# One 512-column matmul for two of the high-part terms of a split-float32 product, on one NeuronCore

## The reference, cut to what matters

```python
def conv_ffn(h, w_up, cw, cb, w_down, prev):
    u = h @ w_up                                   # 1024 -> 2 * 2816
    y, new_prev = causal_dwconv(u, prev, cw, cb)   # 3 taps along the tokens
    g, val = jnp.split(y, 2, axis=-1)
    return (jax.nn.silu(g) * val) @ w_down, new_prev
```

## Time and profile before

| | |
|---|---|
| runs of the kernel before, us | 1524.21, 1524.72, 1529.47 |
| span of the profiled execution, us | 1519.0 |
| granted TensorE clock, mean | 0.971 |
| TensorE matmuls, busy | 12097, 1413.4 us |
| VectorE busy | 976.7 us |
| ScalarE, GpSimd busy | 576.7 us, 638.5 us |

### The profile page before, as it was taken

The page is one execution under the profiler, slowest core; times in us unless marked ns, Lnnn a source line. Parts: engine busy times, 40 slices in busy tenths (PEclk is TensorE's granted clock), DMA queues, the critical chain, the costliest instruction groups (busy, mean ns, idle before and its releaser), DMA issues.

```text
span 1519.0 us, 32537 instructions
## 1 busy us (share of the span) xinstructions
PE 1413.4 (93%) x12097; PEld 1313.9 (86%) x12097; DVE 976.7 (64%) x1658; ACT 576.7 (38%) x1019; POOL 638.5 (42%) x420
## 2 busy tenths in 40 slices
PE   6986978989999999999799989999989999999997
PEld 6984758979999999999699966657889999999997
DVE  5769967576773167765748688753677761376755
ACT  4544354344432133422415235432454431234323
POOL 1586422304444334433177888402223443344430
PEclk9998789989999999999999999999999999999999
DMA  5344364213333232332145769995213233233321
GB/s 173 114 117 79 63 169 123 83 44 85 99 94 98 77 97 83 102 98 75 45 121 164 226 175 308 331 340 157 69 57 97 84 103 90 83 91 88 104 83 62
DMA packets 289082, 180.47 MB, mean 119 GB/s; under 512 B 54248, under 2 KB 274572, under 8 KB 288924
## 3 DMA queue, kind: packets, MB, share of 16 engines
q1 hardware_dynamic: 288412, 179.07, 40.9%
q10 hardware_dynamic: 576, 0.13, 0.0%
HBM read 167.10 MB, written 10.63 MB: 117 GB/s over the span
## 4 chain that ended last, share of the span: by engine, by line
PE 70%; DVE 14%; issue 8%; ACT 2%; SPq 2%; DMA 1%; POOL 1%; DVEq 0%; ACTq 0%; POOLq 0%
PE big L2649 58%; PE big L2715 3%; PE misc L2800 2%; DVE tmp L1261 2%; PE big L2746 2%; DVE y L1738 1%; DVE rstd L1219 1%; DVE x L1744 1%; DVE w_lo L1208 1%; DVE x_lo L1251 1%; SPq L597 1%; PE misc L2770 1%; ACT yc L2506 1%; DVE cp L1261 1%; ACT w_hi L2144 1%
## 5 line engine op out<-in xcount | busy, mean ns | idle before, releaser
L949 POOL TENSOR_TENSOR w_lo<-raw,w_hi 128x1024 fp32r<-128x1024 f32 (+2 forms) x153 | 393.8, 2574 | 708.9 <-ACT w_hi L2144 548.4
L2144 ACT ACTIVATE w_hi<-raw 128x1024 fp32r<-128x1024 f32 (+2 forms) x179 | 198.5, 1109 | 582.1 <-PE big L2649 539.0
L2649 PE MATMUL big<-x_hi,w_hi 128*128 128x264 f32 x1984 | 406.7, 287 | 8.4 <-DVE uc L1827 2.8
L2649 PE MATMUL big<-x_hi,w_lo 128*128 128x264 f32 x1984 | 400.8, 283 | 0.0
L2649 PE MATMUL big<-x_lo,w_hi 128*128 128x264 f32 x1984 | 398.8, 283 | 0.0
L2649 PEld LDWEIGHTS big<-x_hi,w_hi 128*128 128x128 f32 x1984 | 305.9, 189 | 13.1 <-issue 4.7
L2649 PEld LDWEIGHTS big<-x_lo,w_hi 128*128 128x128 f32 x1984 | 305.6, 189 | 0.0
L2649 PEld LDWEIGHTS big<-x_hi,w_lo 128*128 128x128 f32 x1984 | 305.3, 189 | 0.0
L1831 DVE SCALAR_TENSOR_TENSOR yc<-uc,convw,yc 128x512 f32<-128x512 f32 x88 | 136.7, 1554 | 113.2 <-ACT yc L2506 113.2
L2649 PE MATMUL big<-h_hi,w_hi 128*128 128x264 f32 x616 | 125.1, 284 | 6.3 <-DVE h_lo L1846 6.3
L2649 PE MATMUL big<-h_hi,w_lo 128*128 128x264 f32 x616 | 123.9, 282 | 0.0
(11 more groups left out here) (434 smaller groups left out, 2330.8 us busy)
## 6 DMA issues: line engine op xcount, KB each, us to landing
raw<-in_w_up SPq DMA_DIRECT2D x88, 512.0 KB, 3.9
raw<-in_w_down SPq DMA_DIRECT2D x32, 704.0 KB, 4.7
areas<-in_cache_k SPq DMA_DIRECT2D x41, 384.0 KB, 4.5
areas<-in_cache_v SPq DMA_DIRECT2D x41, 384.0 KB, 4.7
raw<-in_w_in SPq DMA_DIRECT2D x16, 512.0 KB, 4.2
raw<-in_w_out SPq DMA_DIRECT2D x16, 512.0 KB, 4.2
raw<-in_w_kv SPq DMA_DIRECT2D x12, 512.0 KB, 4.6
spare<-in_cache_k SPq DMA_DIRECT2D x12, 384.0 KB, 4.5
```

The lines of the kernel that those rows point to most:

```text
L949: pool.tensor_tensor(w_lo[slot][:, 0:kb, :], raw[slot][:, 0:kb, :], w_hi[slot][:, 0:kb, :].bitcast(F32), ALU.subtract).then_inc(lo_made, 1)
L2144: A.activation(w_hi[slot][:, 0:kb, :], raw[slot][:, 0:kb, :], ACT.Copy).then_inc(hi_made, 1)
L2649: ins = pe.matmul(big[2 * slot + b_][:, 0:c1 - c0], w[slot][:, k, :], r[:, c0:c1], start=(k == 0 and n_ == 0), stop=(k == kb - 1 and n_ == 2))
```

## The change

The high and low parts of an activation become one tensor (`x_hl`, `h_hl`, with `x_hi`, `x_lo`, `h_hi`, `h_lo` as its two views, at the same place and of the same size). For the second column part, `w_hi` meets the high and the low part in one matmul of 2 x 256 columns, whose two results stand side by side in the 512 columns of the bank. The `w_lo` term of that part goes on top of the first 256 columns. Per k there are five matmuls in place of six. The two results are added when a panel is read. `product` stays as it was for the memory panels and for `glu`, and `kvf` is unchanged too; the panels of `win0`, `wout0`, the four up and four down phases, `win1`, `kv` and `wout1` take the new form, 164 panels with 1408 k steps. Its core:

```diff
+            def term(slot, n, k, kb, hl):
+                c0, c1 = HALF[0] if n in (0, 2, 3) else HALF[1]
+                o, wide = big[2 * slot + (n in (1, 4))], c1 - c0
+                if n == 1:
+                    return pe.matmul(o[:, 0:2 * wide].rearrange("p (a t) -> p a t", a=2), w_hi[slot][:, k, :],
+                                     hl[:, :, k, c0:c1], start=(k == 0), stop=False)
+                w, part = (w_lo if n > 2 else w_hi), 1 if n == 2 else 0
+                return pe.matmul(o[:, 0:wide], w[slot][:, k, :], hl[:, part, k, c0:c1],
+                                 start=(k == 0 and n == 0), stop=(k == kb - 1 and n > 2))
...
+            LATE = HALF[1][1] - HALF[1][0]
+            def both(slot, dst):
+                src = big[2 * slot + 1][:, 0:2 * LATE].rearrange("p (a t) -> p t a", a=2)
+                return V.tensor_reduce(dst, src, AX.X, ALU.add)
...
                             dve.wait_ge(panel_done, q + 1)
-                            st(V.tensor_tensor(uu[:, 2:266], big[2 * slot][:, 0:264], rstd[:, 0:264], ALU.mult))
-                            V.tensor_tensor(uu[:, 266:2 + NT], big[2 * slot + 1][:, 0:256], rstd[:, 264:NT],
-                                            ALU.mult).then_inc(panel_read, 1)
+                            late = uu[:, 2 + HALF[1][0]:2 + NT]
+                            st(both(slot, late))
+                            st(V.tensor_tensor(uu[:, 2:2 + HALF[0][1]], big[2 * slot][:, 0:HALF[0][1]], rstd[:, 0:HALF[0][1]],
+                                               ALU.mult))
+                            sy(1)
+                            V.tensor_tensor(late, late, rstd[:, HALF[1][0]:NT], ALU.mult).then_inc(panel_read, 1)
```

```diff
-                ins = V.tensor_tensor(dst, dst, src, add) if add else V.tensor_copy(dst, src)
+                if n and add:
+                    for i in range(2):
+                        ins = V.tensor_tensor(dst, dst, big[2 * (q % 2) + 1][:, i * LATE:(i + 1) * LATE], ALU.add)
+                        if i == 0:
+                            do(ins)
+                            sync()
+                elif n:
+                    ins = both(q % 2, dst)
```

More of the change, by code:

```diff
@@ L1780, in copy_out @@
                     dve.wait_ge(panel_done, q + 1)
[L1781 to L1787, removed]
+                    first, late = (y[:, m, c0:c1] for c0, c1 in HALF)
+                    src = big[2 * (q % 2)][:, 0:HALF[0][1]]
+                    high, low = (big[2 * (q % 2) + 1][:, i * LATE:(i + 1) * LATE] for i in range(2))
+                    if add:
+                        do(V.tensor_tensor(late, late, high, ALU.add))
+                        added = own.n
+                        do(V.tensor_tensor(first, first, src, ALU.add))
+                        dve.wait_ge(dve_step, added)
+                        ins = V.tensor_tensor(late, late, low, ALU.add)
+                    else:
+                        do(V.tensor_copy(first, src))
+                        ins = both(q % 2, late)
+                    tell(ins, panel_read, q + 1)
                     for a_ in conv_rows(m) if conv is not None else ():
@@ L2636, in all_read, with joined @@
                     pe.wait_ge(free_, (jobs - n + len(frees) - 1) // len(frees))
+            def term(slot, n, k, kb, hl):
[7 more added lines that the diff above has]
+                                 start=(k == 0 and n == 0), stop=(k == kb - 1 and n > 2))
+            def joined(q, slot, kb, hl, wait_k=None, free=True, each=None):
+                pe.wait_ge(lo_made, q + 1)
+                if free:
+                    pe.wait_ge(panel_read, q - 1)
+                for k in range(kb):
+                    if wait_k is not None:
+                        wait_k(k)
+                    for n in range(5):
+                        ins = term(slot, n, k, kb, hl)
+                    if k == kb - 1:
+                        ins.then_inc(panel_done, 1)
+                    if each is not None:
+                        each(k)
             def product(q, slot, kb, rhs, cols, wait_k=None, free=True, each=None):
@@ L2656, in _, with product_by_halves, phase @@
             xs_ = lambda k: (x_hi[:, k, :], x_lo[:, k, :])
[L2658 removed]
+            def product_by_halves(q, slot, kb, hl, wait_half):
                 pe.wait_ge(lo_made, q + 1)
                 pe.wait_ge(panel_read, q - 1)
[L2662 removed]
+                for b_ in range(2):
                     wait_half(b_)
                     for k in range(kb):
[L2665 to L2668 removed]
+                        for n in ((0, 2, 3), (1, 4))[b_]:
+                            ins = term(slot, n, k, kb, hl)
                 ins.then_inc(panel_done, 1)
[L2671 removed]
+            def phase(name, hl=x_hl, wait_k=None, wait_half=None, first=0, last=0):
                 kb, n, base, _ = PH[name]
@@ L2710, in last_pair @@
                         slot = q % 2
-                        def part(k, n_):
-                            xh, xl = rhs(k)
-                            w, r = ((w_hi, xh), (w_hi, xl), (w_lo, xh))[n_]
-                            return pe.matmul(big[2 * slot + b_][:, 0:c1 - c0], w[slot][:, k, :], r[:, c0:c1],
-                                             start=(k == 0 and n_ == 0), stop=(k == kb - 1 and n_ == 2))
                         if b_ == 0:
@@ L2734, in first_pair @@
                 add = x_stats(name)
-                for b_, (c0, c1) in enumerate(HALF):
+                for b_ in range(2):
                     for p_ in range(2):
@@ L2744, in first_pair @@
                                 x_split(KD * b_ + k)
-                            for n_, (w, r) in enumerate(((w_hi, x_hi), (w_hi, x_lo), (w_lo, x_hi))):
-                                ins = pe.matmul(big[2 * slot + b_][:, 0:c1 - c0], w[slot][:, k, :], r[:, k, c0:c1],
-                                                start=(k == 0 and n_ == 0), stop=(k == KD - 1 and n_ == 2))
+                            for n_ in ((0, 2, 3), (1, 4))[b_]:
+                                ins = term(slot, n_, k, KD, x_hl)
                             if b_ == 0 and p_ == 0 and k == LAST_READ:
@@ L3267, in _ @@
             for m in range(n):
[L3268 removed]
+                joined(base + m, (base + m) % 2, kb, x_hl)
                 if m:
```

102 lines of the change are left out of this document (54 added, 48 removed).

## The result

The changed kernel takes 1667.88 us (median of 4 runs, 1663.67 to 1670.58) where the kernel before took 1524.47 (1523.25 to 1529.47): a ratio of 1.0932, 95% interval 1.09 to 1.0963. It is slower, as forecast, but by 143 us where 103 were forecast, and the time lies above the range. The profiled execution has a span of 1668.4 us, 149.4 above that of before.

The account below looks back on a forecast made before the run. Bound in the up loop: a closed VectorE-ScalarE chain, not TensorE. Span 1519.0 - 7.2 (matmuls) + 98.6 (up loop) + 3.4 (phase ends) + 8 (`kv`) = 1621.8; median 5.7 above, 1628 us, 6.8% slower; range 1572 to 1650.

Parts of the forecast that it names:

- Rival 1: Up loop: the late multiplication is not held up, TensorE's 11.35 us decides; 1513 us, faster; chance 0.13.
- Rival 2: Up loop: only the even `w_lo` holds up the late multiplication; iteration grows 1.29 us, 1576 us in all; chance 0.08.
- Rival 4: Whole kernel: the change doesn't do what it says; at most the matmuls' saving is zero, +7 us; no chance given.
- Three signs: Up loop: VectorE busy above 90%, TensorE's idle before even panels ended by `w_lo`; joined matmul start to start near 225 ns.
- In each phase I count this for nine of eleven iterations.: Four up phases: 2.74 us more in nine iterations each, +98.6 us; first and last iterations counted at nothing.
- The loop's term: Up loop: 4 x 9 x 2.74 = +98.6 us, from iterations growing to 14.27 us.
- I take 11.8, the row of the same kind.: TensorE: joining two 256-column matmuls saves one fixed part of 11.8 ns a k step.
- The 608 steps: Joined k steps outside the up phases and `kv`: 608 x 11.8 ns = -7.2 us.
- saving of 20.6 ns: TensorE, other end of the estimate: a lean joined matmul of 216 ns saves 20.6 ns a k step.
- Ends of the four phases with a norm ... +3.4: Two late readings each on VectorE's chain at phase ends: 2.3 us as additions, 1.1 as copies, +3.4 in all.
- the turns that were put at nothing: Down phases, `win0`, `win1` and the up phases' first and last iterations: no added time forecast.
- rival 3: Up loop: TensorE's idling lowers the granted clock; below 0.79 its panels show, at 0.70 1698 us; chance 0.05.

Follow-up runs that it names:

- e3: The changed kernel with the up loop's reduction `both` issued twice, with a wait between: 1680.33 us, ratio 1.1044.
- e1: The changed kernel with the up loop's late part read out of PSUM in three operations of at most one SBUF input each: 1537.21 us, ratio 1.0097.
- e5: As e1, with the late readings with `rstd` in `win0`, `kv` and `win1` also taken out of PSUM: 1529.56 us, ratio 1.0031.
- e7: Joined matmul only in up phases and down-phase panels read by copies, additions; e1's reading in up loop, rest as before the change: 1523.89 us, ratio 0.9975.
- e6: As e1, but the up loops' joined matmul reads 512 neighbouring columns in one piece (wrong columns, same count): one run, 1533.29 us.
- e2: The kernel before, six matmuls kept; up loop's late part first copied to `uc` in SBUF, then multiplied there: 1650.28 us, ratio 1.0846.
- e4: The changed kernel with each GpSimd `w_lo` subtraction split into two instructions of half the blocks, in every phase: 1586.62 us, ratio 1.0428.

## Why the prediction was right in kind and too small

**Right: the mechanism and the iteration.** The late multiplication is held up by both `w_lo` of an iteration and ends 0.28 us behind them (0.24 was assumed); the odd `w_lo` has moved to the last tap; L1831 (now L1860) runs in 0.75 us. The iteration is 14.32 us against 14.27. The reduction took 0.68 us against 0.69, and e3 shows that its price would not have mattered in the steady loop. Rival 1 fell with the changed kernel itself and its reason, that only operations of 512 and more columns had been seen blocked, fell too: one of 8 columns was stopped for 3 us (below). Rival 2 fell with the odd multiplication's 1.99 us. Rival 4 fell by the page's count of matmuls. Three signs came out otherwise. VectorE is busy for 11.04 of the 14.32 us, 77% and not above 90%, since it still waits twice for ScalarE's tap (1.33 and 1.27 us). The joined matmul takes 231 to 233 ns and not 225 (below). And TensorE's wait before an even panel ends by `panel_read` (L1857) and not by `w_lo`. The two are 0.28 us apart, since the multiplication ends right behind `w_lo`.

**Wrong: "In each phase I count this for nine of eleven iterations."** This is the step that failed most. The loop's term was 98.6 us; 121.0 were measured, 22.4 more. 16.3 of these lie in the last two intervals from `h` to `h` of each phase. In the first up phase the intervals went from 10.78, 11.26 and then 11.53 to 14.3 in all of the first eight. The ninth, counted at 2.74, went from 11.53 to 17.21 us; the tenth, counted at nothing because "the next `w_lo` belongs to the down phase and waits only for `w_hi`", from 12.75 to 13.79. In the other three phases these two agree within 0.2 us. The other 6.1 us are in the first eight: they grow by 2.8 to 2.9 us, and the first two of the phases f = 0 by more (3.6 and 3.1), because they were shorter before than the 11.53 that I took as the base.

What waits only for `w_hi` is not harmless. The first two `w_lo` of the down phase have 11 blocks, and before the change both already ran inside the last iteration and stopped both L1831 there (2.11 and 2.53 us in place of 0.75). GpSimd and then VectorE before the change:

```profile
457.91 3.23 POOL L949 TENSOR_TENSOR w_lo<-raw,w_hi 128x1408 fp32r<-128x1408 f32 x1 [4.03 <-ACT w_hi L2144]
463.38 3.24 POOL L949 TENSOR_TENSOR w_lo<-raw,w_hi 128x1408 fp32r<-128x1408 f32 x1 [2.24 <-ACT w_hi L2144]
```

```profile
459.58 2.11 DVE L1831 SCALAR_TENSOR_TENSOR yc<-uc,convw,yc 128x512 f32<-128x512 f32 x1 [1.10 <-ACT yc L2506]
...
464.64 2.53 DVE L1831 SCALAR_TENSOR_TENSOR yc<-uc,convw,yc 128x512 f32<-128x512 f32 x1 [1.10 <-ACT yc L2506]
```

The same after the change, in the last two iterations of the first up phase:

```profile
485.19 3.29 POOL L949 TENSOR_TENSOR w_lo<-raw,w_hi 128x1408 fp32r<-128x1408 f32 x1 [3.30 <-ACT w_hi L2182]
494.02 3.66 POOL L949 TENSOR_TENSOR w_lo<-raw,w_hi 128x1408 fp32r<-128x1408 f32 x1 [5.54 <-ACT w_hi L2182]
```

```profile
485.49 3.54 DVE L1871 TENSOR_TENSOR hf<-sg,yc 128x520 f32<-128x520 f32 x1
...
494.52 3.18 DVE L1866 SCALAR_TENSOR_TENSOR yc<-convs,convw,yc 128x8 f32<-128x8 f32 x1
```

Before, the first of them started behind the ninth interval (457.91, `h_lo` at 457.10); after, it starts 4.55 us ahead of the interval's end (485.19, `h_hl` at 489.74), because ScalarE makes its `w_hi` straight behind the silu (483.74) where before it waited 3.54 us for TensorE (until 456.45): TensorE is ahead now. It stops `hf`, which takes 0.70 us elsewhere, for 3.54: the ninth interval grows by the steady 2.79 and by these 2.84. In the tenth the second one stops a tap of 8 columns (3.18 us in place of 0.22), about as much as the two L1831 lost there before (2.96 against 3.14 us). The late multiplications are not stopped in it (0.42 us), so nothing hides the two reductions, and their 2 x 0.61 us less 0.18 make the 1.04.

**Wrong in size: "I take 11.8, the row of the same kind."** TensorE's steady k step went from 11.53/16 = 0.7208 us (before) to 0.7150 (e1, e5, e7), so joining saves 5.8 ns and not 11.8. With 3 x 122 + 118.3 ns for the other four, the joined matmul takes 231 ns; read directly in e1, from its start to the next one's, it has a median of 233, above the 225 of the forecast. The working took what lies above 106.7 ns in a 256-column matmul as a fixed part; of those 11.8 ns (118.3 - 106.7 is 11.6, which alters little) about half grow with the columns, since 256 and 512 columns fit 6 ns and 0.44 ns a column, where 1/2.4 is 0.417 and the granted clock was 1.00. e6 shows that it isn't the pattern; why a column takes more is open. The 608 steps give 3.5 us, not 7.2. The Trainium skill's 215.7 ns for 512 columns ("TensorE: Matmul & The Clock Gate", "Wait — 56ns, not 53.3ns?") isn't reached by this stream of float32r matmuls with a weight load each. The section that the prediction names, "Back-to-back issue gap", gives the formula as the gap of an isolated matmul, and some 131 ns at 512 columns for a stream with weight loads, which is further still from the measured 231. By its saving of 20.6 ns the forecast would have been 12.5 - 7.2 = 5.3 us lower, further off.

**Wrong too: "Ends of the four phases with a norm ... +3.4", and the turns that were put at nothing.** Outside the loops the forecast had -7.2 + 3.4 + 8 = +4.2 us; the table gives 28.4. `kv` is about as forecast: +8 there, 6.1 by the table, 7.4 by e1 against e5. Of the 10.3 us in attention and `wout1` about 7 are probably not the change's: e2 and e7, in which this stretch has the code of before, take 246.5 and 246.7 us in it where the profiled execution of before took 239.4. The stretch scatters: e1 takes 241.9 in it, with the code of the changed kernel. The profiled execution of before lay below its median, and those 7 us are about what the spans' difference (149.4) has above the medians' (143.4).

That leaves 28.4 - 7 = 21 us where 4 were forecast. 3.7 of the 17 missing are the matmul's smaller gain; the others are in the turns between the stages, where additions of +3.4 were forecast and some 19 measured (21.4 less the 6.1 of `kv`, with the 3.5 of the matmul added back). About 8 of them come with the slow loop and not with any addition: e2, in which nothing but the up loop's reading is changed, is 8.0 us above before outside the loops, with attention and `wout1` left out (the first iteration of each phase, which I had put at nothing, is in them). The clock has a part too. TensorE after and then before, in `wout1` and in the last stretch, the columns being those of the earlier trace rows:

```profile
1122.00:1215.00 93.00, 84.66 (x505) 76.33 (x505) 57.96 (x96) 36.51 (x65) 21.86 (x10) 0.91 0.24 68
1584.00:1668.00 84.00, 74.75 (x486) 67.33 (x486) 47.61 (x77) 21.64 (x30) 19.31 (x6) 0.90 0.21 65
```

```profile
1043.00:1130.00 87.00, 79.13 (x591) 75.42 (x592) 54.66 (x92) 35.99 (x65) 21.72 (x10) 0.98 0.24 71
1438.00:1519.00 81.00, 71.24 (x564) 68.15 (x564) 46.10 (x68) 21.42 (x30) 19.35 (x6) 0.96 0.22 70
```

The granted clock is a mean between its two levels of 1.2 and 2.4 GHz. Where it falls can be seen in the timeline of TensorE at the start of `wout1` after the change:

```profile
1123.27 0.40 PE L2684 MATMUL big<-x_hl,w_hi 128*128 128x264 f32 x2
1123.51 0.28 PE L2684 MATMUL big<-x_hl,w_lo 128*128 128x264 f32 x1
1123.63 0.59 PE L2684 MATMUL big<-x_hl,w_hi 128*128 128x264 f32 x2
...
1124.23 0.64 PE L2684 MATMUL big<-x_hl,w_hi 128*128 128x264 f32 x2
1124.67 0.42 PE L2684 MATMUL big<-x_hl,w_lo 128*128 128x264 f32 x1
1124.89 0.64 PE L2684 MATMUL big<-x_hl,w_hi 128*128 128x264 f32 x2
```

Three matmuls of 264 columns take 1123.63 - 1123.27 = 0.36 us, then 1124.89 - 1124.23 = 0.66: the lower level, for 3 us, behind the tail of attention with its short operations and waits. In `wout1` this can't be laid to the change: e7, with the code of before there and a fast loop, has 0.92 too. In the last 84 us e1, whose code there is the changed kernel's, takes 81.1 us where the changed kernel takes 84.0 and the kernel before 80.9. So those 3 us come with the slower loop ahead of it, behind which the clock stands at 0.90, and not from the extra additions alone, which cost 0.2 us in e1; e2, with the slow loop and the code of before behind it, takes 82.5 at a clock of 0.94. That is as much as rival 3 has to it: in the loops themselves the granted clock stayed at 0.95 to 0.97, far above the 0.79 from which it decides. How the rest of the turns shares out between the clock, the late readings and the scatter between executions was not settled.

## What to carry to other kernels

Before you move an operand from PSUM to SBUF on VectorE, look at what GpSimd is doing at that moment: with its second input in SBUF too, a multiplication of 0.42 us became one of 1.7 to 2, and it had no slack ahead of it, because the event that frees VectorE also starts GpSimd. Keep one input in PSUM, even at the price of an operation more (e1: four operations of 0.42 us beat three), or cut GpSimd's instruction so that the stop ends sooner (e4). And when a loop's chain grows, count its first and last iterations with it: work that is started by another engine's progress (here the down phase's `w_lo`) then meets other operations than before.

## What the runs showed that was not expected

- A VectorE operation is stopped even if it is tiny: L1866, 8 columns, 0.22 us otherwise, stood for 3.18 us behind a `w_lo` of 3.66.
- The stop ends with GpSimd's instruction, even if the next one follows at once: VectorE's multiplication ended 0.29 us behind the first half, though the second is drawn from 0.04 us before the first one's end (e4), and the second half took 1.46 us where the first took 1.29.
- A 512-column float32r matmul with its own weight load takes 231 ns from start to start, 0.44 ns a column and 6 ns besides, whether its columns lie in one piece or in two (e6).
- A reduction over pairs that are 256 columns apart in a PSUM bank takes 0.684 us for 512 values, the same as a contiguous one, and is not stopped by `w_lo` (e3).
